# Attention scores in four PSUM banks of 384 columns, with the low-key product taken from 64 rows of the array

## What is computed

```python
def windowed_gqa_attention(q, k, v, sink):        # 16 query heads, 4 key heads, 64 wide
    ...
    def block_fn(args):                           # one block of 128 queries
        j, qj, kj, vj = args
        ...                                       # its window: the block before, its own, the one behind
        s = jnp.einsum('bqgrd,bkgd->bgrqk', qj.astype(F32), kj.astype(F32)) * scale + alibi
        s = jnp.where(valid, s, -jnp.inf)
        ...
        p = jax.nn.softmax(jnp.concatenate([s, sink_col], axis=-1), axis=-1)[..., :-1]
        o = jnp.einsum('bgrqk,bkgd->bqgrd', p, vj.astype(F32))
        return o.astype(qj.dtype)
```

## Time and profile before

| what | value |
|---|---|
| median of three runs | 2370.17 us (2369.28 to 2371.48) |
| span of the profiled execution, first to last instruction | 2367.7 us |
| TensorE busy, share of the span | 2338.8 us, 99% |
| VectorE busy | 1551.7 us, 66% |
| ScalarE busy | 908.8 us, 38% |
| GpSimd busy | 1286.5 us, 54% |
| mean granted TensorE clock | 0.999 of 2.4 GHz |

### The profile page before, as it was taken

The page is one execution under the profiler, slowest core; times in us unless marked ns, Lnnn a source line. Parts: engine busy times, 40 slices in busy tenths (PEclk is TensorE's granted clock), DMA queues, the critical chain, the costliest instruction groups (busy, mean ns, idle before and its releaser), DMA issues.

```text
span 2367.7 us, 37099 instructions
## 1 busy us (share of the span) xinstructions
PE 2338.8 (99%) x13702; PEld 2115.4 (89%) x13702; DVE 1551.7 (66%) x2699; ACT 908.8 (38%) x1862; POOL 1286.5 (54%) x1556
## 2 busy tenths in 40 slices
PE   7999999999999999999999999999999999999998
PEld 6888888888888888888888899999999999999887
DVE  6735467554674547755786643999778777965537
ACT  5212443224442244324644112554333434552443
POOL 3365522555225641356453549797455555986676
PEclk9999999999999999999999999999999999999999
DMA  3132211321113311224354443332443434488873
GB/s 140 52 109 90 68 40 27 113 92 50 37 40 107 96 52 32 63 87 130 125 168 158 142 152 119 125 118 90 153 148 130 164 132 138 146 280 274 275 244 121
DMA packets 186956, 285.66 MB, mean 121 GB/s; under 512 B 14344, under 2 KB 126824, under 8 KB 186776
## 3 DMA queue, kind: packets, MB, share of 16 engines
q1 hardware_dynamic: 139320, 241.99, 30.7%
q10 hardware_dynamic: 47456, 41.31, 5.9%
HBM read 203.48 MB, written 79.68 MB: 120 GB/s over the span
## 4 chain that ended last, share of the span: by engine, by line
PE 87%; DVE 7%; DVEq 2%; POOL 1%; ACT 1%; issue 1%; DMA 1%; ACTq 0%
PE ps L3300 15%; PE ps L3302 15%; PE ps L3301 15%; PE ps L3858 3%; PE ps L3859 3%; PE ps L3860 3%; PE ps L3315 3%; PE ps L3311 3%; PE ps L3312 3%; PE ps L3365 3%; PE ps L3367 3%; PE ps L3366 3%; PE ps L3472 2%; PE ps L3567 2%; PE ps L3587 2%; PE ps L3453 1%
## 5 line engine op out<-in xcount | busy, mean ns | idle before, releaser
L3300 PE MATMUL ps<-ht_h,unit_h 128*128 128x512 f32 (+1 forms) x1408 | 503.3, 357 | 1.5 <-POOL unit_l L1403 0.8
L3302 PE MATMUL ps<-ht_h,unit_l 128*128 128x512 f32 (+1 forms) x1408 | 498.5, 354 | 0.0
L3301 PE MATMUL ps<-ht_l,unit_h 128*128 128x512 f32 (+1 forms) x1408 | 498.3, 354 | 0.0
L1381 POOL TENSOR_TENSOR unit_h<-unit_raw,colt 128x256 fp32r<-128x256 f32 x320 | 212.6, 694 | 274.7 <-DMA unit_raw<-w 274.4
L3300 PEld LDWEIGHTS ps<-ht_h,unit_h 128*128 128x128 f32 x1408 | 266.1, 189 | 38.0 <-POOL unit_l L1403 1.9
L3302 PEld LDWEIGHTS ps<-ht_h,unit_l 128*128 128x128 f32 x1408 | 265.9, 189 | 37.6
L3301 PEld LDWEIGHTS ps<-ht_l,unit_h 128*128 128x128 f32 x1408 | 266.1, 189 | 35.1 <-issue 0.2
L1385 POOL TENSOR_TENSOR unit_l<-unit_raw,unit_h 128x256 fp32r<-128x256 f32 x320 | 245.3, 797 | 11.7 <-issue 0.4
L1553 POOL TENSOR_TENSOR unit_l<-unit_raw,unit_h 128x256 fp32r<-128x256 f32 x164 | 158.1, 988 | 91.8 <-DVE unit_raw L2959 91.8
L1553 POOL TENSOR_TENSOR sum_l<-sum_raw,sum_h 128x256 fp32r<-128x256 f32 x132 | 139.4, 1075 | 90.3 <-DVE sum_raw L2966 78.2
L1474 POOL TENSOR_TENSOR v_high<-v_raw,colt 128x256 fp32r<-128x256 f32 x40 | 27.0, 675 | 231.9 <-DVE o_st L2474 231.9
(11 more groups left out here) (429 smaller groups left out, 6448.2 us busy)
## 6 DMA issues: line engine op xcount, KB each, us to landing
unit_raw<-w SPq DMA_DIRECT2D x149, 512.0 KB, 3.7
bw<-exponent_rows_scratch ACTq DMA_DIRECT2D x40, 256.0 KB, 3.6
down_raw<-wdn SPq DMA_DIRECT2D x24, 384.0 KB, 4.0
side_raw<-side_sum_scratch SPq DMA_DIRECT2D x24, 384.0 KB, 6.3
block_raw<-weight_sum_scratch SPq DMA_DIRECT2D x16, 576.0 KB, 4.4
gate_scratch<-g_st SPq DMA_DIRECT2D x28, 256.0 KB, 2.2
stage<-f_scratch SPq DMA_DIRECT2D x28, 256.0 KB, 3.0
side_sum_scratch<-stage SPq DMA_DIRECT2D x14, 512.0 KB, 2.8
```

The costliest lines, as they stand in the source:

```text
L1381: nc.gpsimd.tensor_tensor(unit_h[:, slot, k:k + 2], unit_raw[:, slot, k:k + 2], one_col.unsqueeze(2).to_broadcast([P, 2, P]), ALU.mult)
L3300: mm(out_ap, wh, hi(k + k_first), start=first and k == 0, stop=False, skip_group_check=skip)
L3301: mm(out_ap, wh, lo(k + k_first), start=False, stop=False, skip_group_check=skip)
L3302: ins = mm(out_ap, wl, hi(k + k_first), start=False, stop=last and k == kts - 1, skip_group_check=skip)
```

## The change

Blocks with three key blocks (`WIDE`, `j` = 3 to 8) get a bank for each query head: heads 0, 1 and 2 the first 384 columns of banks 2, 3 and 4, head 3 those of bank 0 or 1, whichever the second of the two dense groups behind the scores will use (`turn_scores_bank`). PE waits for that bank before the second pair of heads (`turn_scores_bank_free`), and before that second dense group for VectorE to have read head 3 (the new count `a_wide`, which shares the semaphore `fr_b12`). VectorE reads the heads in the order 3, 2, 1, 0. Blocks with two key blocks put heads 0 and 2 into bank 2 and heads 1 and 3 into bank 3.

In all blocks the heads are taken in pairs: the two products with `kk_h`, 128 rows each, then the two with `kk_l`, which now take 64 rows each, those that hold the high query parts: rows 0 to 63 for the even head of the pair and 64 to 127 for the odd one. The term (low query) x (low key) falls away.

```diff
-S_AT = [3 * P * r for r in range(4)]
+WIDE = [j for j in range(NB) if j not in (0, NB_A - 1, NB_A, NB - 1)]
...
-    def score_at(j, r):
+    def turn_scores_bank(j, h):
+
+        if h < HEADS - 1:
+            return GROUPS[("M", h + 1, M_BESIDE[j - 1][1])][1]
+        return B_BESIDE[j - 1][1] % 2
+
+    def score_of(j, r, h):
 
         kb = kblocks(j)
-        return S_AT[r] if len(kb) == 3 else 2 * P * r - (kb[0] - j + 1) * P
+        if j in WIDE:
+            return ps[:, 2 + r if r < QPG - 1 else turn_scores_bank(j, h), 0:3 * P]
+        return ps[:, 2 + r % 2, 2 * P * (r // 2):2 * P * (r // 2) + len(kb) * P]
...
-                for r in range(QPG):
-                    V.scalar_tensor_tensor(prob[:, r, a:b], absrel[:, a:b], slope8[:, bass.ds(h * QPG + r, 1)],
-                                           flat[:, score_at(j, r) + a:score_at(j, r) + b], ALU.mult, ALU.add)
+                for r in range(QPG)[::-1]:
+                    last = V.scalar_tensor_tensor(prob[:, r, a:b], absrel[:, a:b], slope8[:, bass.ds(h * QPG + r, 1)],
+                                                  score_of(j, r, h), ALU.mult, ALU.add)
+                    if j in WIDE and r == QPG - 1:
+                        last.then_inc(a_wide, 1)
...
+            def turn_scores_bank_free(j, h):
+
+                if h < HEADS - 1:
+                    bank_free(pe, lambda k: ("M", k + 1, M_BESIDE[j - 1][1]), h)
+                else:
+                    pe.wait_ge(b_mix, B_BESIDE[j - 1][0])
...
                 pe.wait_ge(a_ql, lin(lambda k: NB * k + j + 1, h))
-                for r in range(QPG):
-                    lo = score_at(j, r) + a
-                    while lo < score_at(j, r) + b:
-                        hi = min(score_at(j, r) + b, (lo // 512 + 1) * 512)
-                        k0 = (j - 1) * P + lo - score_at(j, r)
-                        for n, keys in enumerate((kk_h, kk_l)):
-                            ins = mm(ps[:, 2 + lo // 512, lo % 512:lo % 512 + hi - lo], q_st[j > 0][:, r % 2, r // 2],
-                                     keys[:, k0:k0 + hi - lo], start=n == 0, stop=n == 1)
-                        lo = hi
+                keys = slice(kb[0] * P, kb[-1] * P + P)
+                for pair in range(QPG // 2):
+                    if j in WIDE and pair:
+                        turn_scores_bank_free(j, h)
+                    for odd in range(2):
+                        mm(score_of(j, 2 * pair + odd, h), q_st[j > 0][:, odd, pair], kk_h[:, keys], start=True, stop=False)
+                    for odd in range(2):
+                        rows = slice(HD * odd, HD * odd + HD)
+                        ins = mm(score_of(j, 2 * pair + odd, h), q_st[j > 0][rows, odd, pair], kk_l[rows, keys],
+                                 start=False, stop=True)
                 ins.then_inc(a_s_done, 1)
...
-                        for g in M_BESIDE[j]:
+                        for n, g in enumerate(M_BESIDE[j]):
+                            if n == 1 and j + 1 in WIDE:
+                                pe.wait_ge(a_wide, wide_scores(j + 1, h))
...
                         for n in B_BESIDE[j]:
+                            if n == B_BESIDE[j][0] + 1 and j + 1 in WIDE:
+                                pe.wait_ge(a_wide, wide_scores(j + 1, h))
                             branch_m(n)
```

More of the change, by code:

```diff
@@ L736, in build @@
     s_f = [sem("f_stored0"), sem("f_stored1")]
-    fr_b12 = sem("front_last_use_of_b12")
+    a_wide = fr_b12 = sem("scores_beside_dense_groups_read_and_then_front_last_use_of_b12")
     w_sum = sem("w_sums")
@@ L868, in tiles_before, with wide_scores @@
         return sum(len(kblocks(n)) for n in range(j))
-    def score_at(j, r):
-        kb = kblocks(j)
-        return S_AT[r] if len(kb) == 3 else 2 * P * r - (kb[0] - j + 1) * P
+    def turn_scores_bank(j, h):
[3 more added lines that the diff above has]
+    def score_of(j, r, h):
+        kb = kblocks(j)
+        if j in WIDE:
+            return ps[:, 2 + r if r < QPG - 1 else turn_scores_bank(j, h), 0:3 * P]
+        return ps[:, 2 + r % 2, 2 * P * (r // 2):2 * P * (r // 2) + len(kb) * P]
+    def wide_scores(j, h):
+        return len(WIDE) * h + WIDE.index(j) + 1
     def chunk_of(d, i):
@@ L2658, in scores_max @@
                 dve.wait_ge(a_s_done, lin(lambda k: NB * k + j + 1, h))
-                flat = ps[:, 2:5, :].rearrange("p b t -> p (b t)")
                 if j > 0:
                     dve.wait_ge(a_t, lin(lambda k: NB * k + j, h))
-                for r in range(QPG):
-                    V.scalar_tensor_tensor(prob[:, r, a:b], absrel[:, a:b], slope8[:, bass.ds(h * QPG + r, 1)],
-                                           flat[:, score_at(j, r) + a:score_at(j, r) + b], ALU.mult, ALU.add)
+                for r in range(QPG)[::-1]:
[3 more added lines that the diff above has]
+                        last.then_inc(a_wide, 1)
                 dve.drain()
@@ L2952, in block_sums @@
                 else:
-                    dve.wait_ge(fr_b12, 1)
+                    dve.wait_ge(fr_b12, len(WIDE) * HEADS + 1)
                 a11, a22 = block_of(i, "A11")[2], block_of(i, "A22")[2]
@@ L3550, in late_group @@
                 unit_group("A", LATE[n] // 3, LATE[n] % 3, HEADS - 1, before=before)
+            def turn_scores_bank_free(j, h):
[3 more added lines that the diff above has]
+                    pe.wait_ge(b_mix, B_BESIDE[j - 1][0])
             def a_scores(j, h):
                 kb = kblocks(j)
-                a, b = (kb[0] - j + 1) * P, (kb[-1] - j + 2) * P
                 if j in (0, NB_A):
```

## The result

The changed kernel takes 2381.99 us (median of 4 runs, 2380.71 to 2382.65) where the kernel before takes 2370.57 on the same chip (median of 4, three of which are those of the table ahead): ratio 1.005, 95% interval 1.0038 to 1.0061, slower by 11.4 us. The span of the profiled execution grew from 2367.7 to 2379.9 us.

A forecast was written before the change was run, and what follows sets the result against it. PE was taken as the bound, with the scores on the path that sets the end. Gains of 5.5 and 3.2 us against 31.5 lost made +22.8, 2393 us; the forecast's own range was 2376 to 2396, the wider one 2366 to 2398 (0.80).

The forecast's parts named there:

- The four banks: Scores with three key blocks: eight matmuls of 384 columns replace twelve, 0.23 us less a block, 5.5 us gained.
- The price of a switch: Scores on PE, going between 128 and 64 rows: 0.197 us for each of 160 switches, 31.5 us lost.
- Two heads on disjoint rows: Low-key products of a head pair: the second starts 0.11 us after the first, overlapping partly, 3.2 us gained.
- the second rival: Low-key products on disjoint rows overlap wholly, but switches cost: 2384 us at 0.197 each, 2376 at 0.147; chance 0.17.
- The sum: Whole kernel: gained 5.5 + 3.2, lost 31.5, so +22.8 us, 2393 us.
- The new waits: PE's waits for the third head's bank and before the second dense group cost nothing: 0.5 and over 4 us spare.
- Free switches: Low-key products switch rows free: gain 5.5 us without overlap, 17.3 with full overlap, 2364.7 to 2352.9; chance 0.15.
- no overlap: Low-key products of a pair run one behind the other: +26.0 us, or +18.0 at 0.147 a switch; chance 0.18.
- no change: Whole kernel: switches of 0.08 to 0.14 us with full overlap eat the gains, 2365 to 2375 us; chance 0.07.

The follow-up runs named there:

- the run with the banks alone: Changed kernel with the four banks kept and low-key products back on all 128 rows: 2366.14 us against 2369.82 for the kernel before, ratio 0.9985.
- the run with all low products on rows 0 to 63: Changed kernel, high-key products first, then low-key ones for heads 0, 2, 0, 2, odd heads' left out: 2379.07 us, ratio 1.004 to the kernel before.
- The run with one trip: Changed kernel with four high-key products first, then four low-key ones, two switches a block: 2368.02 us, ratio 0.999 to the kernel before.
- the run of one head of the pair: Changed kernel with only the even head's low product on 64 rows, the odd one's on 128 ahead of it: 2392.91 us, ratio 1.0098.

## Why the prediction came out as it did

The side was right, the size twice too large: 2393 was said, 2382 measured, inside the range. By its own steps:

- **The four banks**, 5.5 us gained: right in the attention (5.3 in the run with the banks alone), 3.7 in the time; two us went back elsewhere in the profiled execution.
- **The price of a switch**, 0.197 us, worked out from the 0.147 of transposes on 64 rows and the longer load: right. Two rows of 384 columns give 0.207 and 0.206, one of 256 (from 287.74 to 288.49 us, with three slots of 0.119) gives 0.197, and of the parts 0.09 to 0.10 is waiting and 0.10 to 0.11 the load that lies bare. The rule that changing the mode drains TensorE (the Trainium skill, TensorEngine Tiling (Array Packing), Key Properties) agrees in that the first load starts about 0.1 us late, fp32r or transposes alike; that TensorE is empty by then no row shows. Where transposes follow, the load is the short one and the switch costs 0.15.
- **Two heads on disjoint rows**, 3.2 us gained: this is the term that was mis-sized. It let the second head's load begin 0.11 us after the first's, the spacing of fp32r loads on 128 rows, which it took for that of every load (the transposes on 64 rows, each with a load of its own, start 0.0625 apart in the earlier trace rows). The two loads for disjoint rows run at the same time, so the whole slot is saved, 0.172 and 0.119 a pair: 48 x 0.172 + 32 x 0.119 = 12.1 us. That is the second rival with the forecast's price, 2384. A block with three key blocks takes 1.61 + 0.18 = 1.79 us where 2.05 was said, one with two 0.95 + 0.55 = 1.50 where 1.73 was. The 4 ns between matmuls on disjoint row groups that the Trainium skill states (TensorE: Matmul & The Clock Gate, Part 3) are 3 to 4 ns in the changed kernel; the run with all low products on rows 0 to 63 shows what it is worth, 11 us.
- **The sum.** With that term 31.5 - 5.5 - 12.1 = +13.9; the attention grew by 11.5. The last switch of 24 blocks goes into transposes and costs 0.05 us less, 1.2. That makes 12.7, which is also what the 40 blocks add up to when their scores and the first instruction behind them are read one by one in the two traces. The rest, 1.2, is waiting of PE that was there before and is gone. The first key head had none ahead of its last scores and grew by 3.2; the others grew by 0.3 to 0.5 less. In the second and the third key head it is one wait each for the probabilities, two of the five of the earlier trace rows; the other three come behind the last block's scores, outside this stretch. In the last one it is in the main a dense matmul at 1149.34 us, whose releaser the profile before does not show:

```profile
PE ps L3300 <- issue: 0.7, 1, 0.7
```

So the prediction's reading that PE's other waits lie outside the attention missed one. After the change the list has none of these waits. That they take up what the scores lose is read from one execution of each kernel, not tried by itself.

- **The new waits** cost nothing, as said: neither stands among PE's waits after, and in all 24 blocks the third head starts 0.366 to 0.369 us behind the product before it. The run with one trip shows how near it was, 0.07 us in two blocks.
- **The rivals.** Free switches fell with the rows of the change; no overlap fell with the run of one head of the pair; no change, 2365 to 2375, fell with the time.

## What to carry to other kernels

Count the trips, not the matmuls: going to 64 rows and back costs 0.35 to 0.4 us here, as much as two matmuls of 384 columns, so collect all the 64-row work of a stage behind one switch, and leave it on 128 rows where there are not more than two slots to save. Cutting a product at a bank's end makes pieces of 128 columns that run at the pace of weight loads (0.11 us) and not of their columns (0.053); a bank for each head is worth a new wait if the trace shows that the bank is free by then.

## What was not expected

- Two weight loads for disjoint halves of the rows start 3 to 4 ns apart and take the time of one (0.19 us for both), where loads of 128 rows keep 0.11 us from each other.
- Matmuls of 64 rows do not keep the order of issue across the halves. Issued 384, 384, 256, 256 columns for rows 0 to 63 twice and then 64 to 127 twice, they ran 384 and 256 together, then 256, then 384, in each of the 24 blocks. So for these matmuls the order of the code is not the order on the engine, as the description of the kernel before has it for every engine. The Trainium skill (TensorE: Matmul & The Clock Gate, Part 3) has matmuls strictly in program order; in these runs that did not hold, and the measurement decides. The signal kept the order all the same: in that run the matmul that carries the count for VectorE is the last one issued, of 256 columns, which starts at 350.26 and ends at 350.54 by its row; the trace has the count raised at 350.68, 0.03 us after the end of the one of 384 that ran last (in the changed kernel it comes 0.02 us after the end of the last one).
